# Attention items six deep with the multiplication on GpSimd, and constant matrix products in four kinds of stage

## The chip, the cores and the metric

The kernel runs on one core of one Trainium2 chip. A core has a matrix engine (TensorE, "PE" in the profile), a vector engine (VectorE, "DVE"), an activation engine (ScalarE, "ACT"), a general engine (GpSimd, "POOL") and a queue engine for transfers (SyncE, "SP"). The metric is the device time of one execution in microseconds (us).

## The reference

Two decoder blocks run one after the other on 256 latent tokens of width 1024. The first has two layers (mLSTM with gated linear attention, then RWKV-7, each with a convolutional FFN). The second has a layer of sparse attention with a SwiGLU FFN, and a layer of three-branch attention with a mixture of 8 experts. In both attention layers of the second block, each head does

```
s = q @ k.T * scale                  # 256 queries, up to 256 keys
p = softmax(where(mask, s, NEG))     # float32
o = p @ v
# three-branch layer: o = g0 * o_cmp + g1 * o_slc + g2 * o_win
# (cmp: up to 16 compressed keys; slc and win: up to 256 keys)
```

Everything is float32, with 16 query heads and 4 key/value heads of size 64. All other layers are projections, norms, scans and FFNs, float32 too.

## The kernel before

The program is a sequence of some 45 stages. Each stage is one block (`engines_block`, L204): every engine has its own instruction list, engines meet only by semaphores, and at the end of a block all engines wait for each other (the barrier is line L206).

`attention_stage` (L3653) is called twice: with one branch (16 items) in the sparse layer, and with three branches (48 items) in the other. An item is one query block of 128 rows, one pair of heads and one branch; query block b = 0 comes first for all pairs, and its items see at most 128 keys, those of b = 1 up to 256. The compressed branch has 16 keys in both. Each item passes through these steps:

- PE `score` (L3688): q times k for both heads into one of two PSUM pairs `SC`. It waits until the item two before has been read.
- VectorE `mask` (L3770, L3772): scale and add the mask into `scores` in SBUF, then the negated row maximum into `low`. The second waits for the first through a chain semaphore.
- ScalarE `expo` (L3747): exponential in place for each head, with the row sum into `total`.
- VectorE `norm` (L3780 to L3785): reciprocal of the sum, times the gate (three-branch layer), times a 0/1 mask for the compressed branch, then the whole row times the reciprocal.
- PE `turn` (L3699): transposes of the probabilities into PSUM.
- ScalarE `copy_turned` (L3732): PSUM to `pt`.
- PE `add` (L3711): probabilities times v, summed over branches in PSUM; ScalarE `copy_out` (L3738) stores the sum.

PE's order is written out: score(n), turn(n-2), add(n-3). VectorE's is mask(n), norm(n-1). `scores` has three slots, `low` and `total` have two. GpSimd has no work in the stage.

`norm_stage` (L935) computes an RMS norm, sometimes two in a row. PE sums squares (L1025), and after the reciprocal it spreads the result over all partitions (L1032); then VectorE, ScalarE and GpSimd scale (L1075, L1008, L1061, L1102). `row_stage` (L1426) is an output projection with weights that stream in whole rows; PE's products are L1468. `ffn_up_stage` (L2561) and `swiglu_stage` (L3798) are column projections whose products are L1330. In these three, PE's first product waits until ScalarE and VectorE have cut inputs and weights into two float32r parts.

`st.C("ones")` and `st.const` are constants that stay in SBUF. A plain float32 product gives two MATMUL records in the trace, a transpose one record, a float32r product one.

Of the kernel before, what the change touches and what calls it, by code (L numbers as in the profile page):

```python
# [934 lines left out]
def norm_stage(core, st, jobs, ahead=(), squares=None, early=None, late=None):  # L935
# [7 lines left out]
    with ExitStack() as ctx, core.engines_block() as block:  # L943
# [71 lines left out]
        def _(pe):  # L1015
            for j, job in enumerate(jobs):
# [17 lines left out]
                if j == 0 and late:  # L1034
                    late.multiply(pe)

# [80 lines left out]
        for turn in (early, late):  # L1117
            if turn:
                turn.settle()

# [305 lines left out]
def row_stage(core, st, g, T, rhs, lo, places, store, squares, squared, sums=(), ops_per_row=1.0, sums_from=0):  # L1426
# [7 lines left out]
    with ExitStack() as ctx, core.engines_block() as block:  # L1434
# [22 lines left out]
        def _(pe):  # L1457
            for k in range(K):
# [1102 lines left out]
def ffn_up_stage(core, st, weights, layer, T, sums, n_sums):  # L2561
# [10 lines left out]
    with weights.up_ctx as ctx, core.engines_block() as block:  # L2572
# [22 lines left out]
        @block.tensor  # L2595
        def _(pe):
            for n in range(len(g.tiles)):
                g.multiply(pe, n, x)
# [1054 lines left out]
def attention_stage(core, st, q, branches, out, ahead):  # L3653
# [13 lines left out]
    with ExitStack() as ctx, core.engines_block() as block:  # L3667
        begin_ahead(block, ahead)
        s = core.sb("scores", [P, 3, 2, LAT], ctx=ctx)
        low = core.sb("low", [P, 2, 2], ctx=ctx)  # L3670
        total = core.sb("total", [P, 2, 2], ctx=ctx)
        pt = core.sb("pt", [P, 2, 4, P], ctx=ctx)
        names = ("scored", "masked", "exped", "normed", "turned", "pt_ready", "summed", "out_taken")
        scored, masked, exped, normed, turned, pt_ready, summed, out_taken = (core.counter("at_" + n) for n in names)
        chain = core.counter("vector_chain")
# [4 lines left out]
        def _(pe):  # L3680
            def score(n):
                b, hp, i = items[n]
                br = branches[i]
                if n >= 2:
                    pe.wait_ge(masked.sem, masked.at(n - 1))
# [6 lines left out]
            def turn(n):  # L3692
# [4 lines left out]
                for h in (0, 1):  # L3697
                    for j, (at, w) in enumerate(branches[i].blocks(b)):
                        ins = nc.tensor.transpose(TR[n % 2][0:w, (h * 2 + j) * P:(h * 2 + j + 1) * P], s[:, n % 3, h, at:at + w], st.C("ident"))  # L3699
# [15 lines left out]
            for n in range(N + 3):  # L3715
                if n < N:
                    score(n)
                if 0 <= n - 2 < N:
                    turn(n - 2)
                if 0 <= n - 3:  # L3720
                    add(n - 3)

        @block.scalar
        def _(act):
# [15 lines left out]
            def expo(n):  # L3740
                b, hp, i = items[n]
                act.wait_ge(masked.sem, masked.at(n + 1))
                if n >= 2:
                    act.wait_ge(normed.sem, normed.at(n - 1))
                for h in (0, 1):
                    x = s[:, n % 3, h, 0:branches[i].keys(b)]
                    ins = nc.scalar.activation(x, x, ACT.Exp, bias=low[:, n % 2, h:h + 1], accum_out=total[:, n % 2, h:h + 1])  # L3747
                ins.then_inc(exped.sem, 1)

            for n in range(N + 4):  # L3750
                if 0 <= n - 2 < N:
                    copy_turned(n - 2)
                if n < N:
                    expo(n)
                if 0 <= n - 4 and (n - 4) % B == B - 1:
                    copy_out((n - 4) // B)

        @block.vector
        def _(dve):
            c = Chain(dve, chain)  # L3760

            def mask(n):
# [3 lines left out]
                x = s[:, n % 3, :, 0:K]  # L3766
                dve.wait_ge(scored.sem, scored.at(n + 1))
                if n >= 3:
# [902 lines left out]
```

## Time and profile before

| | us |
|---|---|
| median of 3 runs | 3501.94 (3500.34 to 3508.61) |
| the profiled execution | 3500.28 |
| its span in the profile | 3498.5 |

| engine | busy us | share |
|---|---|---|
| PE | 3126.0 | 89% |
| VectorE | 2504.4 | 72% |
| ScalarE | 1802.0 | 52% |
| GpSimd | 387.2 | 11% |

The busy time counts an instruction from its start to its end, with pipelined matmuls modelled. "PEclk" is the clock that TensorE was granted, as a share of full speed (1.00 is 2.4 GHz, 0.50 is 1.2 GHz). An "idle before" in brackets tells how long the engine stood before the instruction and whose event ended that. The costliest group in the whole program is the expert stage, some 980 us, in which the change has no line.

### The profile page before, as it was taken

To read this page: it belongs to the slowest core of one execution; us is meant where nothing else is said; L and a number is where in the kernel's file an instruction comes from. 1 tells how busy PE (TensorE), PEld (TensorE's weight loads), DVE (VectorE), ACT (ScalarE), POOL (GpSimd) and SP (SyncE) were. 2 spreads that over 40 slices of the span, in tenths; PEclk is the share of its full clock that TensorE was granted. 3 is DMA by queue.
4 is the path that set the end of the run, shared out by engine and by line. 5 is a ranking of instruction groups with operands and counts; after the bars stand their busy time and mean duration, and the time that the engine had idled before them with its cause. 6 is when DMAs were issued, how large, how long until landed. Compare 5 with 4: busy or idle time off the path is not lost. (4 is left out here: it accounts for less than half of the span.)

```text
span 3498.5 us, 67988 instructions
## 1 busy us (share of the span) xinstructions
PE 3126.0 (89%) x27208; PEld 2625.8 (75%) x27208; DVE 2504.4 (72%) x3881; ACT 1802.0 (52%) x3062; POOL 387.2 (11%) x370
## 2 busy tenths in 40 slices
PE   5998888999798898869987899888899999999997
PEld 3774457877673787759975898656789888988996
DVE  4867674449666445577857677566699999999997
ACT  2433233323313665435424444445588888878875
POOL 0000013431000221018300111000000000000000
PEclk8999889999899999979987999868899999999998
DMA  6530033428131000048730798300699999999995
GB/s 233 154 99 1 1 120 122 150 91 298 48 100 24 4 5 4 24 156 272 274 120 25 252 324 303 96 31 26 220 359 376 352 367 351 376 359 360 374 352 197
DMA packets 269600, 647.19 MB, mean 185 GB/s; under 512 B 25453, under 2 KB 123865, under 8 KB 269081
## 3 DMA queue, kind: packets, MB, share of 16 engines
q1 hardware_dynamic: 248457, 567.86, 45.7%
q0 software_dynamic: 20160, 73.41, 5.8%
q8 instruction: 188, 3.08, 0.4%
q10 hardware_dynamic: 720, 2.23, 0.2%
q14 instruction: 75, 0.61, 0.1%
HBM read 642.39 MB, written 1.05 MB: 184 GB/s over the span
## 5 line engine op out<-in xcount | busy, mean ns | idle before, releaser
L4435 DVE TENSOR_TENSOR weights_lo<-raw_ring,weights_hi 128x896 fp32r<-128x896 f32 (+1 forms) x376 | 413.3, 1126 | 50.7 <-ACT weights_hi L4388 40.9
L4388 ACT ACTIVATE weights_hi<-raw_ring 128x896 fp32r<-128x896 f32 (+1 forms) x376 | 366.9, 986 | 90.7 <-PE bank_pair L4358 89.3
L4358 PE MATMUL bank_pair<-weights_hi,expert_x_hi 128*128 128x448 f32 x1024 | 294.7, 369 | 5.1 <-DVE weights_lo L4435 5.1
L4358 PE MATMUL bank_pair<-weights_hi,expert_x_lo 128*128 128x448 f32 x1024 | 292.6, 367 | 0.0
L4358 PE MATMUL bank_pair<-weights_lo,expert_x_hi 128*128 128x448 f32 x1024 | 292.3, 367 | 0.0
L4435 DVE TENSOR_TENSOR weights_lo<-H,weights_hi 128x896 fp32r<-128x896 f32 (+1 forms) x240 | 264.5, 1133 | 23.6 <-ACT weights_hi L4388 14.7
L4388 ACT ACTIVATE weights_hi<-H 128x896 fp32r<-128x896 f32 (+1 forms) x240 | 236.8, 990 | 68.8 <-PE bank_pair L4358 68.8
L2652 DVE SCALAR_TENSOR_TENSOR conv<-bank_pair,vec,conv 128x189 f32<-128x189 f32 (+3 forms) x396 | 138.5, 428 | 146.5 <-ACT conv L2612 146.5
L4358 PEld LDWEIGHTS bank_pair<-weights_hi,expert_x_hi 128*128 128x128 f32 x1024 | 189.9, 188 | 21.4 <-issue 5.0
L4358 PEld LDWEIGHTS bank_pair<-weights_lo,expert_x_hi 128*128 128x128 f32 x1024 | 192.8, 188 | 16.6
L4358 PEld LDWEIGHTS bank_pair<-weights_hi,expert_x_lo 128*128 128x128 f32 x1024 | 192.9, 188 | 16.5
L1330 PE MATMUL bank_pair<-Y_parts,const_parts 128*128 128x256 f32 (+1 forms) x592 | 145.9, 330 | 9.3 <-DVE H_parts L1375 9.3
L344 PE MATMUL bank_pair<-x_hi,ring_hi 128*128 128x256 f32 (+1 forms) x352 | 117.5, 334 | 36.6 <-DVE x_lo L2769 16.4
L4358 PE MATMUL bank_pair<-weights_hi,hidden_hi 128*128 128x512 f32 x448 | 138.8, 391 | 0.0
L4358 PE MATMUL bank_pair<-weights_hi,hidden_lo 128*128 128x512 f32 x448 | 138.1, 390 | 0.0
L4358 PE MATMUL bank_pair<-weights_lo,hidden_hi 128*128 128x512 f32 x448 | 138.1, 389 | 0.0
L4435 DVE TENSOR_TENSOR weights_lo<-const,weights_hi 128x896 fp32r<-128x896 f32 (+1 forms) x120 | 133.2, 1132 | 2.6
L4388 ACT ACTIVATE weights_hi<-const 128x896 fp32r<-128x896 f32 (+1 forms) x120 | 119.0, 992 | 25.9 <-PE bank_pair L4358 25.3
L620 DVE SCALAR_TENSOR_TENSOR mod_sums_ada<-mod_ring_ada,act,mod_sums_ada 128x1024 f32<-128x1024 f32 x84 | 119.6, 1428 | 6.1 <-DMA mod_ring_ada<-in_w_ada 6.1
L1330 PEld LDWEIGHTS bank_pair<-Y_parts,const_parts 128*128 128x128 f32 x592 | 101.8, 190 | 21.2 <-DVE const_parts L1310 9.6
L1104 POOL TENSOR_SCALAR Y<-H,vec 128x256 f32<-128x256 f32 x2 | 1.8, 916 | 1046.5 <-DVE H L1075 1046.5
L344 PE MATMUL bank_pair<-x_lo,ring_hi 128*128 128x256 f32 (+1 forms) x352 | 115.9, 329 | 0.0
(798 smaller groups left out, 8302.0 us busy)
## 6 DMA issues: line engine op xcount, KB each, us to landing
raw_ring<-in_moe_w_gate SPq DMA_DIRECT2D x72, 896.0 KB, 6.9
raw_ring<-in_moe_w_up SPq DMA_DIRECT2D x64, 896.0 KB, 7.0
ring_up<-in_ffn_w_up SPq DMA_DIRECT2D x110, 512.0 KB, 4.3
raw_ring<-in_moe_w_down SPq DMA_DIRECT2D x48, 1024.0 KB, 7.3
mod_ring_ada<-in_w_ada POOLq DMA_DIRECT2D x84, 512.0 KB, 6.4
H<-in_moe_w_up SPq DMA_DIRECT2D x48, 896.0 KB, 7.1
ring_down<-in_ffn_w_down SPq DMA_DIRECT2D x66, 512.0 KB, 6.3
H<-in_moe_w_down SPq DMA_DIRECT2D x32, 1024.0 KB, 7.1
```

The source lines that it names most:

```text
L344: ins = self.core.nc.tensor.matmul(self.banks[o][:, 0:moving.shape[1]], lhs, moving, start=(s == self.first[o] and k == 0 and i == 0), sto ...
L620: ins = self.core.nc.vector.scalar_tensor_tensor(total, tile, scale, total, ALU.mult, ALU.add)
L1104: nc.gpsimd.tensor_scalar(job.dst(q)[:, h], work[j][:, q, h], job.scale(q, h), None, ALU.mult)
L1330: ins = self.core.nc.tensor.matmul(self.bank(it, o)[:, 0:T], w, y, start=s == self.begin[o] and k == 0 and a == 0, stop=s == self.end[o] a ...
L2652: ins = nc.vector.scalar_tensor_tensor(out, shifted, tap(w, 2 * it + o), out, ALU.mult, ALU.add)
L4358: ins = nc.tensor.matmul(banks[half][:, 0:b - a], x, w[:, a:b], start=start and i == 0, stop=stop and i == 2)
L4388: nc.scalar.activation(hi[:, u % CUTS, 0:n].bitcast(F32R), raw_part(u), ACT.Copy).then_inc(cut.sem, 1)
L4435: nc.vector.tensor_tensor(lo[:, u % CUTS, 0:n].bitcast(F32R), raw_part(u)[:, 0:n], hi[:, u % CUTS, 0:n], ALU.subtract).then_inc(parted.sem, 1)
```

## The change

Attention: six `scores` slots, four each of `low` and `total`. PE's order becomes score(n), turn(n-5), add(n-6). VectorE's order becomes shift(n), invert(n-2), lowest(n), gate(n-2), each with a semaphore of its own. The last multiplication goes to GpSimd. ScalarE copies the result out ahead of the exponential. For b = 0, a product of constants with 256 columns goes to PE ahead of each item's scores, into columns of the PSUM pair that are unused. Two products with 512 columns open the stage.

Elsewhere: a product of 512 columns opens the PE list of `row_stage`, `ffn_up_stage` and `swiglu_stage`; `jobs[-1].items // 2` of them end the PE list of `norm_stage` (2 for 256 tokens, 4 for 512). Nothing reads their results.

```diff
+def keep_busy(core, st, bank, n, cols=slice(0, 512)):
+    for _ in range(n):
+        core.nc.tensor.matmul(core.bank(bank)[:, cols], st.C("ones"), st.const[:, cols], start=True, stop=True)
...
@@ norm_stage, end of PE's list
+            keep_busy(core, st, 5, jobs[-1].items // 2)
...
@@ row_stage, ffn_up_stage, swiglu_stage, start of PE's list
+            keep_busy(core, st, 7, 1)
...
@@ attention_stage
-        s = core.sb("scores", [P, 3, 2, LAT], ctx=ctx)
-        low = core.sb("low", [P, 2, 2], ctx=ctx)
-        total = core.sb("total", [P, 2, 2], ctx=ctx)
+        TURN_LAG = 5
+        SLOTS, FACTORS, NORM_LAG = TURN_LAG + 1, 4, 2
+        s = core.sb("scores", [P, SLOTS, 2, LAT], ctx=ctx)
+        low = core.sb("low", [P, FACTORS, 2], ctx=ctx)
+        total = core.sb("total", [P, FACTORS, 2], ctx=ctx)
...
                 if n >= 2:
-                    pe.wait_ge(masked.sem, masked.at(n - 1))
+                    pe.wait_ge(shifted.sem, shifted.at(n - 1))
+                if b == 0:
+                    keep_busy(core, st, n % 2 * 2, 1, slice(256, 512))
...
-            for n in range(N + 3):
+            keep_busy(core, st, 7, 2)
+            for n in range(N + TURN_LAG + 1):
                 if n < N:
                     score(n)
-                if 0 <= n - 2 < N:
-                    turn(n - 2)
-                if 0 <= n - 3:
-                    add(n - 3)
+                if 0 <= n - TURN_LAG < N:
+                    turn(n - TURN_LAG)
+                if 0 <= n - TURN_LAG - 1:
+                    add(n - TURN_LAG - 1)
...
@@ scalar
-                if n >= 2:
-                    act.wait_ge(normed.sem, normed.at(n - 1))
+                if n >= FACTORS:
+                    act.wait_ge(normed.sem, normed.at(n - FACTORS + 1))
...
-            for n in range(N + 4):
-                if 0 <= n - 2 < N:
-                    copy_turned(n - 2)
+            for n in range(N + TURN_LAG + 2):
+                if 0 <= n - TURN_LAG < N:
+                    copy_turned(n - TURN_LAG)
+                if 0 <= n - TURN_LAG - 2 and (n - TURN_LAG - 2) % B == B - 1:
+                    copy_out((n - TURN_LAG - 2) // B)
                 if n < N:
                     expo(n)
-                if 0 <= n - 4 and (n - 4) % B == B - 1:
-                    copy_out((n - 4) // B)
...
@@ vector
+            for n in range(N + NORM_LAG):
+                if n < N:
+                    shift(n)
+                if n >= NORM_LAG:
+                    invert(n - NORM_LAG)
+                if n < N:
+                    lowest(n)
+                if n >= NORM_LAG:
+                    gate(n - NORM_LAG)
+
+        @block.gpsimd
+        def _(pool):
+            def norm(n):
+                b, hp, i = items[n]
+                br = branches[i]
+                K = br.keys(b)
+                x, r = s[:, n % SLOTS, :, 0:K], total[:, n % FACTORS]
+                pool.wait_ge(inverted.sem, inverted.at(n + 1))
                 if br.gate is not None:
+                    pool.wait_ge(gated.sem, gated.at(n_gated(n + 1)))
                 if br.some is not None:
+                    pool.wait_ge(kept.sem, kept.at(n_kept(n + 1)))
-                nc.vector.tensor_tensor(x, x, r.unsqueeze(2).to_broadcast([P, 2, K]), ALU.mult).then_inc(normed.sem, 1)
+                nc.gpsimd.tensor_tensor(x, x, r.unsqueeze(2).to_broadcast([P, 2, K]), ALU.mult).then_inc(normed.sem, 1)
+
+            for n in range(N):
+                norm(n)
```

`shift` is the first half of the old `mask` and `lowest` the second; `invert` and `gate` are the parts of the old `norm` without its last line.

## Rows read from the trace of the kernel before

**Rows 1.** Windows: busy us per engine (instructions), granted clock, DMA share, GB/s.

```profile
2300.00:2345.00 45.00, 42.63 (x228) 23.36 (x228) 31.44 (x129) 28.25 (x123) 0.00 (x0) 0.50 0.13 48
2345.00:2408.00 63.00, 50.96 (x352) 30.07 (x352) 45.35 (x133) 38.05 (x138) 0.00 (x0) 0.77 0.00 1
```

**Rows 2.** Waits from 2300 to 2408 us: total, times, longest.

```profile
ACT pt L3732 <- PE bank_pair L3699: 32.1, 45, 1.5
```

**Rows 3.** Timeline of PE, first block, second attention stage: start, length, instructions.

```profile
2312.30 0.80 PE L3688 MATMUL bank_pair<-k_slc,q 64*128 64x128 f32 x4
2313.03 0.69 PE L3699 MATMUL bank_pair<-const,scores 128*128 128x128 f32 x2
2313.64 0.70 PE L3711 MATMUL bank_pair<-pt,v_slc 128*64 128x128 f32 x4
2314.27 0.80 PE L3688 MATMUL bank_pair<-k_win,q 64*128 64x128 f32 x4
```

**Rows 4.** Timeline of PE, second block, second attention stage, clock 1.00.

```profile
2389.02 0.43 PE L3711 MATMUL bank_pair<-pt,vc 16*64 16x128 f32 x4
2389.38 0.70 PE L3688 MATMUL bank_pair<-k_slc,q 64*128 64x256 f32 x4
2390.01 0.66 PE L3699 MATMUL bank_pair<-const,scores 128*128 128x128 f32 x4
2390.60 0.66 PE L3711 MATMUL bank_pair<-pt,v_slc 128*64 128x128 f32 x8
2391.19 0.70 PE L3688 MATMUL bank_pair<-k_win,q 64*128 64x256 f32 x4
```

**Rows 5.** Timeline: where both attention stages start, change block and end.

```profile
1889.40 1.23 PE L3688 MATMUL bank_pair<-kd,q 64*128 64x128 f32 x8 [17.49 <-PEq L206]
...
1903.23 1.23 PE L3688 MATMUL bank_pair<-kd,q 64*128 64x256 f32 x4
...
1926.46 0.42 ACT L1371 ACTIVATE x_hi<-Y 128x256 fp32r<-128x256 f32 x1 [0.28 <-PEq L206]
...
2300.90 0.61 PE L3688 MATMUL bank_pair<-kc,q 64*128 64x16 f32 x4 [4.55 <-PEq L206]
...
2344.75 0.61 PE L3688 MATMUL bank_pair<-kc,q 64*128 64x16 f32 x4
...
2407.16 0.42 ACT L1371 ACTIVATE x_hi<-Y 128x256 fp32r<-128x256 f32 x1 [0.29 <-PEq L206]
```

**Rows 6.** Timeline of ScalarE and VectorE, second block, first attention stage.

```profile
1916.68 0.60 ACT L3732 ACTIVATE pt<-bank_pair 128x512 f32<-128x512 f32 x1 [0.26 <-PE bank_pair L3699]
...
1917.97 0.69 DVE L3770 SCALAR_TENSOR_TENSOR scores<-bank_pair,keep 128x512 f32<-128x512 f32 x1
...
1919.49 0.69 DVE L3785 TENSOR_TENSOR scores<-scores,total 128x512 f32<-128x512 f32 x1
1920.10 0.68 DVE L3770 SCALAR_TENSOR_TENSOR scores<-bank_pair,keep 128x512 f32<-128x512 f32 x1
```

**Rows 7.** GpSimd's products elsewhere: by form (count, busy, mean), and ns min/median/max.

```profile
L3240 POOL TENSOR_TENSOR kappa<-rw_k,kappa 128x256 f32<-128x256 f32 x16 | 11.7, 730 | 1.3
...
L1097 POOL TENSOR_TENSOR X<-X,H x6: 1272/1655/1665, 921.1 to 1775.3; 128x512 f32<-128x512 f32 x6
```

**Rows 8.** Weight loads between records of plain float32 products 512 wide; clock there.

```profile
428.66 0.34 PEld L2193 LDWEIGHTS bank_pair<-den,const 128*128 128x128 f32 x1 [0.52 <-issue]
429.51 0.34 PEld L2193 LDWEIGHTS bank_pair<-den,const 128*128 128x128 f32 x1 [0.52 <-issue]
...
427.70:430.00 2.30, 2.30 (x3) 1.11 (x4) 0.50 0.00 0
```

**Rows 9.** A norm's end, an ffn-up stage's first window, a row stage's first product.

```profile
1556.56 1.97 PE L1032 MATMUL bank_pair<-norm_root,const 128*128 128x64 f32 x8 [1.02 <-DVE norm_root L1044]
...
1562.00:1569.60 7.60, 5.06 (x24) 5.09 (x25) 5.20 (x11) 6.44 (x13) 1.93 (x1) 0.50 0.65 194
...
1928.27 0.55 PE L1468 MATMUL bank_pair<-x_hi,X_parts 128*128 128x256 f32 x1 [2.40 <-DVE X_parts L1499]
```

More of the change, by code:

```diff
@@ L3668, in attention_stage @@
         begin_ahead(block, ahead)
-        s = core.sb("scores", [P, 3, 2, LAT], ctx=ctx)
-        low = core.sb("low", [P, 2, 2], ctx=ctx)
-        total = core.sb("total", [P, 2, 2], ctx=ctx)
+        TURN_LAG = 5
[3 more added lines that the diff above has]
+        total = core.sb("total", [P, FACTORS, 2], ctx=ctx)
         pt = core.sb("pt", [P, 2, 4, P], ctx=ctx)
-        names = ("scored", "masked", "exped", "normed", "turned", "pt_ready", "summed", "out_taken")
-        scored, masked, exped, normed, turned, pt_ready, summed, out_taken = (core.counter("at_" + n) for n in names)
-        chain = core.counter("vector_chain")
+        names = ("scored", "shifted", "masked", "exped", "inverted", "gated", "normed", "turned", "pt_ready", "summed", "out_taken", "kept")
+        scored, shifted, masked, exped, inverted, gated, normed, turned, pt_ready, summed, out_taken, kept = (core.counter("at_" + n) for n in names)
+        n_gated = lambda n: sum(branches[i].gate is not None for _, _, i in items[:n])
+        n_kept = lambda n: sum(branches[i].some is not None for _, _, i in items[:n])
         SC = [core.psum[i].rearrange("p (h s) -> p h s", h=2) for i in (0, 1)]
@@ new lines, in shift, with lowest @@
+                nc.vector.scalar_tensor_tensor(s[:, n % SLOTS, :, 0:K], SC[n % 2][:, :, 0:K], HD ** -0.5, br.neg[:, b, 0:K].unsqueeze(1).to_broadcast([P, 2, K]),
+                                               ALU.mult, ALU.add).then_inc(shifted.sem, 1)
+            def lowest(n):
+                b, hp, i = items[n]
+                dve.wait_ge(shifted.sem, shifted.at(n + 1))
+                nc.vector.tensor_reduce(low[:, n % FACTORS], s[:, n % SLOTS, :, 0:branches[i].keys(b)], AX, ALU.max, negate=True).then_inc(masked.sem, 1)
@@ new lines, in invert, with gate @@
+            def invert(n):
+                b, hp, i = items[n]
+                br = branches[i]
+                r = total[:, n % FACTORS]
+                dve.wait_ge(exped.sem, exped.at(n + 1))
+                nc.vector.reciprocal(r, r).then_inc(inverted.sem, 1)
+            def gate(n):
+                b, hp, i = items[n]
+                br = branches[i]
+                r = total[:, n % FACTORS]
+                dve.wait_ge(inverted.sem, inverted.at(n + 1))
+                if br.gate is not None:
+                    nc.vector.tensor_tensor(r, r, br.gate[:, b, 2 * hp:2 * hp + 2], ALU.mult).then_inc(gated.sem, 1)
+                if br.some is not None:
+                    K = br.keys(b)
+                    x = s[:, n % SLOTS, :, 0:K]
+                    nc.vector.tensor_tensor(x, x, br.some[:, b, 0:K].unsqueeze(1).to_broadcast([P, 2, K]), ALU.mult).then_inc(kept.sem, 1)
```

33 lines of the change are left out of this document (11 added, 22 removed).

## The prediction

> **What bounds the kernel now.** I read the stage windows first, since the share of PE over the whole run mixes stages with different limits. Two stretches hold the attention stages. In them PE is busy nearly all the time while its granted clock is 0.50, the lower of its two levels (1.2 GHz), for the whole first block of queries of the second stage; over the second block it averages 0.77 [rows 1]. ScalarE's largest wait there is for PE's transposes, 32.1 us [rows 2]. So in the first block PE is the limit, at half its speed.
>
> The timeline of PE shows the cadence of one 128-key item: scores 0.73 us, transposes 0.61, product with v 0.63, then the next scores, 1.97 us together, none of them after a wait on another engine [rows 3]. At the upper level (2.4 GHz) the same line-up in the second block reads: a 4-record product 0.36, 256-wide scores 0.63, four transposes 0.59, an 8-record product 0.59 [rows 4]. There PE no longer leads: VectorE takes 2.13 us per item without a gap, of which the multiplication by the reciprocal sum is 0.61 (1919.49 to 1920.10), and ScalarE needs 1.87 of it, its 0.26 us wait taken off [rows 6]. The first attention stage runs from 1889.40 to 1926.46, its first 256-wide scores at 1903.23: 13.8 and 23.2 us. The second runs from 2300.90 to 2407.16, its second block from 2344.75: 43.9 and 62.4 us [rows 5].
>
> **The change, part by part.**
>
> *GpSimd multiplies.* VectorE loses 0.61 us per 256-key item (2.13 becomes about 1.5) and the wait between shift and minimum. GpSimd, idle here until now, gets 128x256 and 128x512 products. The nearest rows are 0.73 us for 128x256 and 1.27 to 1.66 us for 128x512 [rows 7]; I take 1.5. For a triple of the second block (16, 256 and 256 keys) that is about 0.4 + 2 x 1.5 = 3.4 us, at most 3.8, beneath what PE will need (below). So it leaves the path. If the cover were gone, a 128x512 product of 2.2 us or more would set the pace.
>
> *Six items deep.* The cycle scores, shift, minimum, exponential, reciprocal, product, transpose now has five items of slack, so PE finds its inputs ready. Its queue still holds all three steps in order: score(n), turn(n-5), add(n-6). The added waits are VectorE's on the shift of the same item (two instructions later, met) and GpSimd's on the reciprocal; behind GpSimd's stand only further products. What is late next is PE itself, with ScalarE close.
>
> *256-column constants in the first block.* 32 products, 8 + 24. Plain fp32 records 512 wide follow at 0.85 us (428.66 to 429.51) with clock 0.50, and a product is two such records [rows 8]: 512 columns cost 1.71 us at the lower level and 0.85 at the upper, 256 columns 0.85 and 0.43. They stand on PE's path: nothing hides them. What they may buy is the clock. At the upper level a 128-key item costs PE 0.42 (0.63 less 0.21 for 128 columns) + 0.37 (0.59 less two transposes at 0.11) + 0.36 = 1.15 us, plus 0.43 = 1.58, against 1.97 now. At the lower level it would be 1.97 + 0.85 = 2.82.
>
> *Opening of attention, 2 x 512 columns.* Nothing hides these either, as the first scores used to start 0.1 us after the barrier: 2 x 1.71 = 3.4 us twice. ScalarE's table load lies beside them.
>
> Second stage, at the upper level from shortly after the opening. First block: opening 3.5; five items with scores and constants only, 5 x 0.95; one with transposes, 1.2; 18 x 1.58 (the 16-key items somewhat less, so 1.52), 27.4; 1.5 for the first 3 us still at half speed. Sum 38.3 against 43.9, saves 5.6. Second block, per triple on PE: scores 0.37 + 0.63 + 0.63, transposes 0.37 + 0.59 + 0.59, products 0.36 + 0.59 + 0.59 = 4.72 us, or 1.57 per item; I take 1.6 since ScalarE needs nearly as much (1.87 twice and about 0.9 once, less two copies of the result at 0.25, 4.2 per triple). 24 x 1.6 - 1.5 (the first transposes still belong to short items) + 7.6 for draining six items = 44.5 against 62.4, saves 17.9. Together 23.5. First stage: first block 3.5 + 4.75 + 1.2 + 2 x 1.58 + 1.5 = 14.1 against 13.8, costs 0.3; second block 5 x 1.56 + 3 x 1.87 (ScalarE) + 7.7 = 21.1 against 23.2, saves 2.1. Attention saves 25.3 in all; I allow 2 us for hand-overs between engines of nearly equal pace, and take 23.
>
> *Stage openings* (row, ffn-up and swiglu stages, 512 columns). The row stage behind the first attention starts at 1926.4 and its first product at 1928.27, after a wait for VectorE's cut [rows 5, 9], so 1.71 us of constants fits; where it doesn't, 0.1 us is lost. The gain is a stage that starts at the upper clock. In the ffn-up stage from 1562.0 the clock is 0.50 for 7.6 us, PE working 5.06 of them [rows 9]: up to 2.5 us of gain, where the next tiles come in time. About ten stages qualify, but several start on saturated DMA. I take 6 us, bounds 0 and 12.
>
> *Norm ends* (512 columns, 2 or 4 times). PE's last spread matmuls end about 3.5 us before the next stage in the latent norms (1556.56 + 1.97 against 1562.0) [rows 9]. 2 x 1.71 us behind them end within some tenths of that, after which the drain follows: 0 to 0.4 us for each of seven norms at the lower clock (the same length of tail is in the other norms that feed a latent stage). I take 2, bounds 0 and 3.
>
> Sum: -23 - 6 + 2 = -27 us; the openings' gain is the least certain term, so I shade it to -26. The profiled execution took 3500.28 us (span 3498.5); it becomes 3474.3. The median of the runs shown is 1.7 us above that execution, so 3476.
>
> A rule of the Trainium skill speaks against the clock step. The rows show the clock low while PE issues transposes in a third of its steps [rows 1, 3]. "TensorE: Matmul & The Clock Gate", section Part 4 on PE-mode transpose, says that transposes don't count as activity for the clock. By that rule the new second block, with no constants in it, could fall back although PE is never idle; this is the first rival's mechanism. No row tells the two apart.
>
> The same product on GpSimd took from 1.27 to 1.66 us [rows 7]. "GPSIMD Engine Reference", section Specifications, puts contention down to VectorE instructions with two SBUF inputs. What VectorE keeps here reads one large SBUF input and PSUM, so by the rule the lower end holds; by the row, the upper. Either is under PE's 4.7 us per triple, so only the chance of the second rival moves.
>
> **The rivals.**
>
> 1. *The constants cost and the clock stays low* (slower). Mechanism: PE in the first blocks. For it: these stretches have held 0.50 for 44 us although PE never waits [rows 1, 3]. Against: the clock does rise once 256-wide scores come [rows 1], and the constants are denser than those. Price: 32 x 0.85 = 27 us, 7 us of openings, norm ends 2, while the second block keeps its present mixture and gains little, about 4: 3500 + 32 = 3534. It decides from the point where less than half of the first block runs at the upper level: half and half means (2.82 + 1.58) / 2 = 2.2 against 1.97, a loss of 7 us there.
>
> 2. *GpSimd or ScalarE sets the pace.* For it: [rows 6, 7], 1.87 and up to 1.66 against PE's 1.57. If every item of the second blocks took 1.9, 24 x 0.3 = 7 us of the gain go, with 2 in the short first items: 3485.
>
> 3. *The clock switches to and fro*, as it does now in the second block. First blocks give nothing or lose a little, second blocks gain 12, openings little: 3491 to 3500, say 3495.
>
> 4. *More than forecast*: openings and norms bring their full 12, and constants partly lie in waits. 3463.
>
> **How the numbers follow.** Forecast 0.62, its own range 3468 to 3484; rival 1 0.07, rival 2 0.11, rival 3 0.10, rival 4 0.10. The range from 3461 to 3494 leaves out rival 1, half of rival 3 and the far ends. A difference of 0.3% (10.5 us) is about what a measurement of this kernel tells from no change. Faster by more: the forecast, rivals 2 and 4 and a little of 3, 0.86. Within 0.3%: most of rival 3, 0.07. Slower: rival 1, 0.07.
>
> **What would show each step.** In the windows, PE's clock near 1.0 from a few us after each attention opening to its end; scores to scores about 1.5 to 1.6 us per item in both blocks of the second stage, and that stage about 83 us long; VectorE with waits for PE in the second block, where it now has none; GpSimd 128x512 products between 1.2 and 1.7 us. The openings are right if the 1562 stage's first tile passes PE in half the time. The prediction is wrong if a window of the first block still reads 0.50, or if GpSimd's products are what PE's transposes wait for.

## The result and the profile after

The changed kernel took 3476.44 us (median of 4 executions, 3468.64 to 3477.95), the kernel before 3505.28 us (4 executions): ratio 0.9915, interval 0.9898 to 0.9932. Measured again, beside three other versions, it took 3473.0 (6 executions) against 3502.16 (11), ratio 0.9905, interval 0.9888 to 0.9922. The ratios here and below are the recorded ones; the two medians alone give 0.9918 and 0.9917. The forecast was 3476, its range 3461 to 3494. The profiled execution took 3477.95 us (span 3476.1).

First the windows of the second attention stage after the change, to be held against [rows 1] (same columns): the opening, the rest of the first block with the first items of the second, and what follows.

```profile
2304.70:2308.70 4.00, 3.89 (x5) 1.85 (x6) 0.00 (x0) 1.28 (x1) 0.00 (x0) 0.50 0.66 220
2308.70:2345.00 36.30, 36.30 (x246) 20.18 (x244) 18.48 (x95) 24.80 (x114) 9.90 (x21) 1.00 0.09 35
2345.00:2389.00 44.00, 42.44 (x381) 25.65 (x382) 29.46 (x113) 37.31 (x145) 20.44 (x28) 1.00 0.01 2
```

The last but two column is the granted clock: 0.50 in the opening, then 1.00 to the end, where it was 0.50 and 0.77 before. PE is busy in 36.30 of 36.30 us and 42.44 of 44.00 us: the second block, where it was idle for 12 of 63 us, is now bound by PE too.

ScalarE's wait for PE's transposes, 32.1 us in [rows 2], is down to 8.1 (waits of the stage: total, times, longest):

```profile
ACT pt L3749 <- PE bank_pair L3715: 8.1, 20, 0.8
```

PE's cadence in the first block, against [rows 3] (start, length, instruction):

```profile
2328.64 0.70 PE L1128 MATMUL bank_pair<-const 128*128 128x256 f32 x2
2329.27 0.49 PE L3704 MATMUL bank_pair<-k_win,q 64*128 64x128 f32 x4
2329.70 0.39 PE L3715 MATMUL bank_pair<-const,scores 128*16 128x128 f32 x2
2330.01 0.44 PE L3727 MATMUL bank_pair<-pt,v_win 128*64 128x128 f32 x4
2330.38 0.70 PE L1128 MATMUL bank_pair<-const 128*128 128x256 f32 x2
```

From constant to constant it is 1.74 us, where an item took 1.97. In it the constant takes 0.63 us (2328.64 to 2329.27) and the kernel's own work 1.11 (1.16 where the transposes are of 128 keys). Next the second block, against [rows 4]:

```profile
2364.31 0.70 PE L3704 MATMUL bank_pair<-k_slc,q 64*128 64x256 f32 x4
2364.94 0.66 PE L3715 MATMUL bank_pair<-const,scores 128*128 128x128 f32 x4
2365.53 0.66 PE L3727 MATMUL bank_pair<-pt,v_slc 128*64 128x128 f32 x8
2366.11 0.70 PE L3704 MATMUL bank_pair<-k_win,q 64*128 64x256 f32 x4
```

One 256-key item follows the other in 1.80 us, with no step waiting. VectorE over the same time (against [rows 6], in brackets the idle time before and what ended it):

```profile
2365.06 0.69 DVE L3784 SCALAR_TENSOR_TENSOR scores<-bank_pair,seen 128x512 f32<-128x512 f32 x1 [0.81 <-PE bank_pair L3704]
2365.66 0.15 DVE L3797 RECIPROCAL total<-total 128x2 f32<-128x2 f32 x1
2365.78 0.69 DVE L3790 TENSOR_REDUCE low<-scores 128x2 f32<-128x512 f32 x1
2366.39 0.15 DVE L3805 TENSOR_TENSOR total<-total,gates 128x2 f32<-128x2 f32 x1
2366.86 0.69 DVE L3784 SCALAR_TENSOR_TENSOR scores<-bank_pair,seen 128x512 f32<-128x512 f32 x1 [0.33 <-PE bank_pair L3704]
```

It has no large multiplication any more, and it waits for PE's scores, 0.81 and 0.33 us here. GpSimd's products (against [rows 7]; groups by form over both attention stages, with count, busy us and mean ns):

```profile
L3833 POOL TENSOR_TENSOR scores<-scores,total 128x512 f32<-128x512 f32 x24 | 25.0, 1042 | 13.0 <-DVE total L3805 9.6 <-DVE total L3797 3.4
L3833 POOL TENSOR_TENSOR scores<-scores,total 128x256 f32<-128x256 f32 x24 | 14.7, 614 | 129.6 <-DVE total L3797 112.6 <-DVE total L3805 17.1
```

Where each attention stage starts and ends, against [rows 5]. Each fence shows the first constant product of a stage: the first attention stage, the row stage behind it, the second attention stage:

```profile
1890.63 1.19 PE L1128 MATMUL bank_pair<-const 128*128 128x512 f32 x1 [17.25 <-PEq L206]
```

```profile
1925.78 1.10 PE L1128 MATMUL bank_pair<-const 128*128 128x512 f32 x2 [0.62 <-PEq L206]
```

```profile
2304.81 1.19 PE L1128 MATMUL bank_pair<-const 128*128 128x512 f32 x1 [5.33 <-PEq L206]
```

From barrier to barrier the first attention stage went from 37.1 to 35.2 us and the second from 106.3 to 84.1: 24.1 us less. In a second profile of the changed kernel they are 35.2 and 84.0.

The first 7.6 us of the ffn-up stage that began at 1562.0, against [rows 9]:

```profile
1567.60:1575.20 7.60, 6.36 (x44) 5.59 (x45) 5.20 (x11) 7.25 (x14) 1.92 (x1) 0.97 0.64 195
```

There are 44 records (two of them the constant's) instead of 24, and a clock of 0.97 instead of 0.50; the stage is 2.1 us shorter, 133.6 for 135.7. Not all of this can be booked for the constants: over the profiles of this study that have them both here and at the end of the norm ahead, the stage takes 133.6 us in seven and 135.0 in four, and it takes 134.9 in constants_only, which has neither.

Stages without an edit differ between profiles too: the one from 1136.8 takes 343.9 us before, 346.4 after, and from 335.9 to 346.4 over all profiles of this study. All stages but the two of attention add up to 3355.1 us before and 3356.9 after, and to anything from 3339.8 to 3365.0 over the 14 profiles. So the total of one execution doesn't settle 5 us. Below, stages are compared one by one, and the totals that carry an argument are those of several executions.

### The profile page after: what moved, and what is told of

Its sections match the earlier page's. It is cut to its first block and busy times, and to the rows that moved or that the text cites. A ratio compares the mean times of both kernels' runs of the same rounds, so it can differ in the third digit from the quotient of the medians.

```text
span 3476.1 us, 68320 instructions
## 1 busy us (share of the span) xinstructions
PE 3149.8 (91%) x27352; PEld 2620.2 (75%) x27352; DVE 2464.0 (71%) x3817; ACT 1799.4 (52%) x3062; POOL 431.4 (12%) x434
## 5 line engine op out<-in xcount | busy, mean ns | idle before, releaser
L4483 DVE TENSOR_TENSOR weights_lo<-raw_ring,weights_hi 128x896 fp32r<-128x896 f32 (+1 forms) x376 | 413.2, 1125 | 51.0 <-ACT weights_hi L4436 41.3
L4436 ACT ACTIVATE weights_hi<-raw_ring 128x896 fp32r<-128x896 f32 (+1 forms) x376 | 366.9, 986 | 91.1 <-PE bank_pair L4406 89.5
L4483 DVE TENSOR_TENSOR weights_lo<-H,weights_hi 128x896 fp32r<-128x896 f32 (+1 forms) x240 | 264.4, 1132 | 23.3 <-ACT weights_hi L4436 14.3
L344 PE MATMUL bank_pair<-x_hi,ring_hi 128*128 128x256 f32 (+1 forms) x352 | 117.9, 335 | 26.6 <-DVE x_lo L2780 12.9
L1128 PE MATMUL bank_pair<-const 128*128 128x512 f32 (+1 forms) x144 | 82.4, 689 | 45.4 <-PEq L206 45.4
```

Source lines behind the costliest of these rows:

```text
L344: ins = self.core.nc.tensor.matmul(self.banks[o][:, 0:moving.shape[1]], lhs, moving, start=(s == self.first[o] and k == 0 and i == 0), sto ...
L1128: core.nc.tensor.matmul(core.bank(bank)[:, cols], st.C("ones"), st.const[:, cols], start=True, stop=True)
L4436: nc.scalar.activation(hi[:, u % CUTS, 0:n].bitcast(F32R), raw_part(u), ACT.Copy).then_inc(cut.sem, 1)
L4483: nc.vector.tensor_tensor(lo[:, u % CUTS, 0:n].bitcast(F32R), raw_part(u)[:, 0:n], hi[:, u % CUTS, 0:n], ALU.subtract).then_inc(parted.sem, 1)
```

## The experiments

Lengths are from barrier to barrier in the profiled execution, in us. "First" and "second" are the two attention stages. The constants in the other stages are in all versions but the kernel before and constants_only; one_opening and no_norm_ends leave out some or all of the norm ends.

| kernel | depth | product on | constants in attention | first | second |
|---|---|---|---|---|---|
| before | 3 | VectorE | none | 37.1 | 106.3 |
| constants_only | 3 | VectorE | both | 39.1 | 107.1 |
| old_depth | 3 | GpSimd | both | 39.5 | 114.5 |
| three_deep | 3 | GpSimd | both | 75.7 | 229.2 |
| multiply_on_vector | 6 | VectorE | both | 36.6 | 88.3 |
| after, and again | 6 | GpSimd | both | 35.2, 35.2 | 84.1, 84.0 |
| no_first_block | 6 | GpSimd | opening | 32.2 | 93.1 |
| no_opening | 6 | GpSimd | ahead of scores | 45.4 | 116.9 |
| no_constants, no_constants_5 | 6 | GpSimd | none | 34.8, 36.5 | 83.7, 89.6 |
| one_opening | 6 | GpSimd | first stage's opening | 32.2 | 83.4 |
| no_norm_ends | 6 | GpSimd | first stage's opening | 32.2 | 89.5 |
| rest_only | 3 | VectorE | none | 38.2 | 110.7 |

**no_first_block: openings without the constants ahead of the scores.**

```diff
-                if b == 0:
-                    keep_busy(core, st, n % 2 * 2, 1, slice(256, 512))
```

> Changed kernel without the 256-column constants ahead of the first block's scores (opening pair kept). The second attention stage took 84.1 us with them. Theory A, the constants must be there all along the first block: the clock drops to 0.50 soon after the opening and PE's 128-key cadence is again 1.9 us or more, so 18 x (1.95 - 1.74) = 4 us longer, 88 us or above. Theory B, once the clock is up, PE's own dense work holds it: no constants to pay, each of 24 items 0.5 to 0.6 us shorter, stage at 71 to 74 us, clock 1.0 throughout. First attention stage, 35.2 us with them: A 35 to 37, B 31 to 32.

One execution: 3470.75 us; first stage 32.2, second 93.1. (The kernel before took 3494.89 beside this one, no_opening, no_constants and multiply_on_vector, one execution each.) The windows of the second stage, from its start:

```profile
2287.00:2291.00 4.00, 3.95 (x8) 1.44 (x8) 0.00 (x0) 1.28 (x1) 0.00 (x0) 0.50 0.65 226
2291.00:2295.00 4.00, 3.23 (x31) 2.28 (x32) 3.53 (x18) 2.97 (x17) 0.85 (x2) 0.93 0.73 300
2295.00:2346.00 51.00, 50.45 (x256) 26.74 (x256) 24.06 (x116) 32.29 (x142) 14.49 (x27) 0.50 0.00 1
```

The opening did lift the clock (0.93), and then it fell and stayed at 0.50 for 51 us in which PE was busy for 50.45. So in the 48-item stage it took the constants ahead of the scores to hold the clock (one profile without them, all profiles of six-deep kernels with both kinds at 1.00). In the 16-item stage it didn't: without them that stage is 3.0 us shorter, in this profile and in two more below.

**no_opening: only the constants ahead of the scores.**

```diff
-            keep_busy(core, st, 7, 2)
             for n in range(N + TURN_LAG + 1):
```

> Changed kernel without the two 512-column constants at the attention opening, those in the first block kept. Theory A (the first block's constants alone raise the clock): the clock is up within some 5 to 7 us, the stage saves the 3.4 us of the opening and pays up to 2.5 us for more work at half speed: 81 to 84 us. Theory B (the opening is what raises it): the clock stays at 0.50 over the first block at 2.8 us per item, stage over 105 us. First attention stage 32 to 35 by A, over 43 by B.

One execution took 3504.66 us, all of the gain gone; first stage 45.4, second 116.9. Its windows:

```profile
2297.10:2343.00 45.90, 45.87 (x174) 23.92 (x176) 13.60 (x69) 19.37 (x84) 7.32 (x15) 0.50 0.12 47
2343.00:2413.90 70.90, 69.64 (x452) 38.66 (x452) 34.74 (x139) 44.68 (x173) 22.93 (x33) 0.72 0.00 1
```

The same constants that held the clock at 1.00 left it at 0.50 when it started there, and then cost more, at the lower clock: 1.15 us each (2326.43 to 2327.58) for 0.63. This is the mechanism of the prediction's first rival, and it comes true when the opening is absent. Its price was too high: it had the total 32 us above the kernel before, and here it is 10, since the second block, which it had gaining 4 us, takes 51.2 for 62.4 even so.

**no_constants: depth and GpSimd alone.**

```diff
-                if b == 0:
-                    keep_busy(core, st, n % 2 * 2, 1, slice(256, 512))
...
-            keep_busy(core, st, 7, 2)
```

> Changed kernel with no constants in attention at all, only the order six deep and the multiplication on GpSimd. Theory A (constants are needed for the clock in the first block): clock 0.50 over it at 1.9 us per item, 44 us for it as before, and second block at about 1.55 us: 43 us; stage 87 us, first attention stage 35 us. Theory B (PE kept fed is enough to raise it): clock rises inside the first block, stage under 78 us.

One execution took 3465.55 us, with stages of 34.8 and 83.7: as short as with the constants. The same kernel again:

> The changed kernel without any constants inside attention (no opening, none ahead of first-block scores); the other stages keep theirs. Theory 1 (the gain is depth and GpSimd; the constants in attention pay for their own time and no more): the attention stages come to 34 to 36 and 83 to 86 us, and the whole is level with the changed kernel within 4 us, either side, ratio to before 0.990 to 0.992. Theory 2 (they cost more than they bring, as one look of 3465.6 suggests): 6 to 10 us below the changed kernel, ratio 0.988 to 0.990. Theory 3 (they hold the clock on most executions and one look missed the bad ones): 5 us or more above the changed kernel, ratio 0.993 or more.

3475.57 us (5 executions), ratio 0.9912, interval 0.9896 to 0.9928, level with the changed kernel. The stages in its profile took 36.5 and 89.6. These are two profiles of one kernel, 6 us apart in one stage. The windows of the second stage, in the first profile and then in the other:

```profile
2292.50:2337.00 44.50, 44.15 (x234) 24.46 (x236) 21.83 (x110) 29.88 (x133) 11.74 (x24) 0.50 0.14 48
2337.00:2376.20 39.20, 37.88 (x344) 23.08 (x342) 25.97 (x100) 33.04 (x125) 18.59 (x24) 0.99 0.01 2
```

```profile
2297.70:2333.00 35.30, 35.01 (x191) 20.09 (x192) 17.23 (x91) 24.74 (x111) 9.63 (x20) 0.50 0.16 60
2333.00:2387.20 54.20, 52.92 (x388) 30.30 (x386) 30.71 (x117) 38.77 (x146) 20.62 (x28) 0.78 0.01 2
```

PE in the first of the two profiles, in the first block and where the second block begins:

```profile
2310.18 0.80 PE L3702 MATMUL bank_pair<-k_slc,q 64*128 64x128 f32 x4
2310.91 0.69 PE L3713 MATMUL bank_pair<-const,scores 128*128 128x128 f32 x2
2311.52 0.70 PE L3725 MATMUL bank_pair<-pt,v_slc 128*64 128x128 f32 x4
2312.15 0.80 PE L3702 MATMUL bank_pair<-k_win,q 64*128 64x128 f32 x4
...
2330.93 0.61 PE L3702 MATMUL bank_pair<-kc,q 64*128 64x16 f32 x4
```

An item of the first block takes 1.97 us (2310.18 to 2312.15), exactly as in [rows 3]: depth doesn't speed it. The block's scores are done after 38.4 us all the same (2292.5 to 2330.93, and 38.4 in the other profile), where the kernel before takes 43.9. Mostly that is because the transposes and products of three items more than before (three at 1.24 us) are put off into the second block, and PE stands 0.2 us at the start instead of 1.4. With constants the block takes 41.3. The second block then takes 45.3 us in one profile (to the end at 2376.2) and 51.2 in the other, by when the clock rises: 44.9 or 58.7 us after the stage began, which is 6.5 or 20.3 us into the block. It takes 42.8 in the changed kernel, with constants, and 62.4 in the kernel before. So constants cost 2.9 us in the first block and give 2.5 to 8.4 in the second, and the stage comes out at 84.1 and 84.0 with them, 83.7 and 89.6 without. What depth brings, beyond work put off, lies in the second block.

**multiply_on_vector: depth and constants, with the product back on VectorE.**

```diff
+                nc.vector.tensor_tensor(x, x, r.unsqueeze(2).to_broadcast([P, 2, K]), ALU.mult).then_inc(normed.sem, 1)
...
-                nc.gpsimd.tensor_tensor(x, x, r.unsqueeze(2).to_broadcast([P, 2, K]), ALU.mult).then_inc(normed.sem, 1)
```

> Changed kernel with the multiplication by the reciprocal sums on VectorE again, behind the gate, rest as it is. Theory A (taking it off VectorE matters in the second block): VectorE then needs about 3.9 + 2 x 0.61 + 0.2 = 5.3 us per triple against PE's 4.6, so the second block grows by 8 x 0.7 = 5 to 6 us, stage 89 to 90 us; first block unchanged. Theory B (depth alone did it, VectorE has room): stage within 1 us of 84.1.

One execution took 3491.72 us; the stages are 1.4 and 4.3 us longer than in the changed kernel. VectorE in the second block:

```profile
2385.23 0.68 DVE L3784 SCALAR_TENSOR_TENSOR scores<-bank_pair,seen 128x512 f32<-128x512 f32 x1
2385.83 0.15 DVE L3797 RECIPROCAL total<-total 128x2 f32<-128x2 f32 x1
2385.94 0.69 DVE L3790 TENSOR_REDUCE low<-scores 128x2 f32<-128x512 f32 x1
2386.55 0.15 DVE L3805 TENSOR_TENSOR total<-total,gates 128x2 f32<-128x2 f32 x1
2386.73 0.69 DVE L3816 TENSOR_TENSOR scores<-scores,total 128x512 f32<-128x512 f32 x1
2387.34 0.68 DVE L3784 SCALAR_TENSOR_TENSOR scores<-bank_pair,seen 128x512 f32<-128x512 f32 x1
```

There is no gap: VectorE sets 2.11 us per 256-key item (2385.23 to 2387.34) against PE's 1.80. So VectorE's relief is worth 5.7 us in both stages together.

**constants_only: the kernel before with attention's constants.**

```diff
+                if b == 0:
+                    keep_busy(core, st, n % 2 * 2, 1, slice(256, 512))
...
+            keep_busy(core, st, 7, 2)
             for n in range(N + 3):
```

> The kernel before, with the attention constants alone: two 512-column products open the stage and one of 256 columns stands ahead of each first-block score. Order, slots and VectorE's multiplication are as before. Theory 1 (the 24 us come from depth and from the multiplication on GpSimd; constants buy a clock that here PE cannot use): the clock is near 1.00, but second block stays at VectorE's 2.13 us per 256-key item and the first block at 1.8 us or more, so the second attention stage takes 98 to 106 us (106.3 before), the first 37 to 39 (37.1 before), and the whole is 0 to 8 us below the kernel before. Theory 2 (the clock alone carries much of the gain): second stage 90 to 95 us, first 35 or less, whole 13 us or more below. Theory 3 (constants cost and the clock stays at 0.50): second stage over 120 us.

One execution: 3506.61 us, where the kernel before took 3491.14 to 3510.76 (17 executions), stages 39.1 and 107.1. The second stage's windows behind its opening:

```profile
2309.20:2345.00 35.80, 34.46 (x234) 18.75 (x233) 25.90 (x105) 23.20 (x103) 0.00 (x0) 1.00 0.09 35
2345.00:2412.00 67.00, 53.95 (x393) 31.95 (x392) 49.69 (x152) 41.51 (x153) 0.00 (x0) 0.85 0.00 1
```

The clock is 1.00 and 0.85 and the stage isn't shorter. In the second block PE is busy in 54 of 67 us and VectorE in 50, so neither is full. They wait for each other (waits from 2310 to 2400: total, times, longest; L3711 is the transposes, L3798 the product on VectorE, L3783 the shift, L3700 the scores):

```profile
PE bank_pair L3711 <- DVE scores L3798: 10.4, 12, 1.3
DVE scores L3783 <- PE bank_pair L3700: 21.7, 27, 5.1
```

That is the chain of one item. In the first block the higher clock pays for the constants and no more: 45.4 us for 43.9. So the clock bought with constants is worth nothing to the stage as a whole (the old form without them takes 106.3 us here and 110.7 in a second profile), which is the first of the expectation's theories, a little beyond its ranges (98 to 106 us, and a total 0 to 8 us below the kernel before).

**three_deep and old_depth: the changed kernel with three slots.** The first only cuts the turn lag; the second also takes the reciprocal one item behind the shift.

```diff
-        TURN_LAG = 5
+        TURN_LAG = 2
...
-        SLOTS, FACTORS, NORM_LAG = TURN_LAG + 1, 4, 2
+        SLOTS, FACTORS, NORM_LAG = TURN_LAG + 1, 4, 1
```

> The changed kernel with a turn lag of 2 in place of 5, so three score slots as in the kernel before; GpSimd's multiplication, the split waits and the constants stay. Theory 1 (depth is what lets PE run without waits, since the chain shift, minimum, exponential, reciprocal, product of one item now has two more hand-overs): PE waits for GpSimd's product at the transposes, 2.1 us or more per item of the second block, second attention stage 95 to 105 us against 84.1, first 37 to 40 against 35.2, whole 3488 to 3500. Theory 2 (taking the multiplication off VectorE was enough, depth is spare): second stage 84 to 87 us, whole within 5 us of the changed kernel.

One execution took 3666.75 us, far outside both theories; the stages take 75.7 and 229.2. VectorE, GpSimd and PE in the second stage show why:

```profile
2419.82 0.42 DVE L3784 SCALAR_TENSOR_TENSOR scores<-bank_pair,seen 128x256 f32<-128x256 f32 x1 [4.05 <-PE bank_pair L3704]
...
2420.91 0.61 POOL L3833 TENSOR_TENSOR scores<-scores,total 128x256 f32<-128x256 f32 x1 [4.38 <-DVE total L3805]
2421.58 0.69 PE L3715 MATMUL bank_pair<-const,scores 128*128 128x128 f32 x2 [1.81 <-POOL scores L3833]
...
2422.82 1.22 PE L1128 MATMUL bank_pair<-const 128*128 128x256 f32 x2
...
2423.97 0.80 PE L3704 MATMUL bank_pair<-k_win,q 64*128 64x128 f32 x4
...
2424.82 0.42 DVE L3784 SCALAR_TENSOR_TENSOR scores<-bank_pair,seen 128x256 f32<-128x256 f32 x1 [4.05 <-PE bank_pair L3704]
```

Read it as a ring: the shift of one item lets VectorE go on to the reciprocal two items back, then GpSimd multiplies, PE transposes, adds, issues the constant and the next scores, and the next shift can start, 5.00 us later. With a reciprocal two items behind and a transpose two items behind, every item closes this ring alone. PE is busy in 142 of the stage's 229 us, and its clock is 0.51 over them, constants or not, so PE's own part of the ring, 3.2 of the 5.0 us here, runs at the lower level too.

> The changed kernel with the depth of the kernel before: turn lag 2 (three score slots) and the reciprocal one item behind the shift, in place of two; GpSimd's multiplication and all constants stay. With the turn lag alone cut to 2 the second attention stage took 229 us, 4.8 us per item, since score(n), shift(n), reciprocal(n-2), product(n-2), transposes(n-2) and score(n+1) made one loop. Here that loop spans two items. Theory 1 (depth carries most of the gain; GpSimd alone, with a chain longer by two hand-overs, brings little): about 2.0 to 2.3 us per item, second attention stage 96 to 110 us, first 38 to 41. Theory 2 (the 229 us came from the order alone, and GpSimd with the old depth is as good as with six items): second stage 84 to 89 us, first 35 to 37.

One execution took 3510.48 us (the kernel before beside it 3504.99), stages 39.5 and 114.5: the first theory, and a little beyond its range in the second stage (96 to 110 was expected). Even with a fit order, GpSimd at the old depth gains nothing; a transpose in the second block still comes behind a wait for the product:

```profile
2399.15 1.11 PE L3715 MATMUL bank_pair<-const,scores 128*128 128x128 f32 x4 [1.27 <-POOL scores L3833]
```

With constants in all four, the table makes a square: three slots and VectorE 107.1, three slots and GpSimd 114.5, six and VectorE 88.3, six and GpSimd 84.1. The step to six is worth 30 us with the product on GpSimd, where lags and slots alone differ. With it on VectorE it is worth 19, but there the three-slot kernel also has the old order on VectorE and the old waits (PE waits for the minimum and not for the shift), and no run parts these from the depth. GpSimd is worth 4 us with depth. That it costs 7 without is not shown: the clock over the second block was 0.69 there for 0.83 in constants_only, and the next experiment shows what such a difference does to that block.

**rest_only: the openings and norm ends elsewhere, with the attention stage of before.** In code, `attention_stage` is put back.

> The changed kernel with the old attention stage: only the 512-column products at the starts of row, ffn-up and swiglu stages and at the ends of the norms are added to the kernel before. The prediction's terms for them: 6 us gained by openings, 2 us lost at norm ends, together 4 us faster. Theory 1 (stage lengths of one profile: openings gain 8 to 9 us in ffn-up, row and router stages, norm ends cost 5, the norm whose 512-column pair starts behind a late product alone 3.9): 1 to 6 us faster, ratio 0.998 to 1.000. Theory 2 (the openings' gain in that profile was chance, the norm ends' cost is not): 2 to 6 us slower, ratio 1.0005 to 1.002.

It took 3495.13 us (12 executions) against 3500.57 (17), ratio 0.9978, interval 0.9964 to 0.9993: 0.0022 x 3500 = 7.7 us faster, between 2 and 13 (5.4 by the two medians). The sign is that of the first theory, the size at the upper end of its 1 to 6 us or a little beyond. Its attention stages, with the same instructions as before, took 38.2 and 110.7 us for 37.1 and 106.3. The difference is in the second blocks: 66.8 us at a mean clock of 0.68 in the second stage, where the kernel before has 62.4 at 0.77. So one profile of the old form is uncertain by 5.5 us in both stages together, and attention's gain may be that much higher than the 24.1 above.

**one_opening and no_norm_ends: versions meant to beat both.** Both have depth and GpSimd, and the opening only in the attention stage with one branch. The first leaves the norm ends out where a norm has a `late` product, the second leaves them all out.

```diff
-            keep_busy(core, st, 5, jobs[-1].items // 2)
+            if not late:
+                keep_busy(core, st, 5, jobs[-1].items // 2)
...
+            if B == 1:
+                keep_busy(core, st, 7, 2)
```

> A version meant to beat both: no constants ahead of scores, the opening only in the first attention stage (one branch), and no constants at the ends of those norms that hold a late product (the one from 2165.1 lost 3.9 us to them). Sum from stage lengths against the changed kernel: first attention 32.2 for 35.2, second about as now, that norm 14 for 17.7, so 6 to 7 us less: 3468 to 3471 where the changed kernel stands at 3476, ratio to before 0.989 to 0.991. Rival: those stage lengths were the clock's chance in single profiles, and the version is level with the one without constants in attention.

> The same, with no constants at the end of any norm. If they only cost (stage lengths: 1.1 us ahead of swiglu, 3.9 in the late norm, 0.1 to 0.5 elsewhere), this is 1 to 2 us below the version that keeps them in the other norms. Rival: they keep the clock for the stage behind, and this one is 2 us or more above it.

> The changed kernel itself on the same chip as the three versions above, for a direct comparison: ratio to before 0.990 to 0.993, as in the first measurement.

Against 3502.16 us for the kernel before: one_opening 3474.25, ratio 0.9914 (0.9896 to 0.9932); no_norm_ends 3479.63, 0.9926 (0.9912 to 0.994); the changed kernel 3473.0, 0.9905 (0.9888 to 0.9922). None beats it, and the intervals don't part the three. Nothing bears out the expectation that norm ends only cost. That the norm from 2165.1 had lost 3.9 us to its constants was wrong: it takes from 13.8 to 20.6 us over the profiles, and 17.5 in one_opening, which has none there. What norm ends bring shows in the ffn-up stage from 534.3. It takes 250.97 or 250.98 us in all ten profiles with constants at the end of the norm ahead of it, and 253.27 in the four without them, two of which have the stage's own opening. The window of its first 4 us, after:

```profile
539.71:543.71 4.00, 2.30 (x7) 1.35 (x8) 3.25 (x6) 3.91 (x7) 0.00 (x0) 1.00 0.53 157
```

and in one_opening:

```profile
532.56:536.56 4.00, 3.25 (x5) 1.55 (x6) 3.25 (x6) 3.91 (x7) 0.00 (x0) 0.50 0.59 161
```

With the norm end the stage begins at 1.00; with the opening alone it is at 0.50, as before. So the gain booked for the opening belongs here to the norm's end. Half of it is lost again in the next stage (from 787.6), which takes 128.9 us in the same ten profiles and 127.7 to 127.9 in the four: the two stages together gain 1.0 to 1.3 us.

## Why the prediction was right, step by step

- **What bounds.** The reading was right for the first block (PE, without waits, at half clock) and half right for the second. There the rows were read as VectorE's pace; at three slots it was just as much the chain of one item, since constants_only keeps 107.1 us with PE idle for 13 of 67 us and VectorE for 17. [rows 1] had the sign of it: VectorE, the third figure, is busy in 45.35 of 63 us.
- **First blocks.** Second stage: 41.3 us (2304.7 to the second block's first scores at 2346.03) against 38.3 forecast. The forecast saving of 5.6 was 2.6. The term that was too small is the 256-column constant, 0.63 us and not 0.43: 24 x 0.2 = 4.8 us. Halving for the columns was the step that failed; halving for the clock was right, as records with 512 columns follow each other at 0.43 us at clock 1.00 (940.31 to 940.74, a norm's end) and 0.85 at 0.50. The item's own work was 1.11 us, for which 1.15 was worked out. Against it stands the 1.5 us for work at half speed, which came to nothing: the clock is 1.00 from 2308.8, before the first scores. The opening took 3.8 us of the stage for 3.5, as no_first_block shows (2286.97 to the scores at 2290.74); in the changed kernel the first scores come 0.6 us later, behind the first item's constant. First stage: 14.3 against 14.1.
- **Second blocks.** They took 42.8 us against 44.5, and 20.8 against 21.1. Three items take 4.62 us on PE (4.72 worked out), and ScalarE, busy for 37 of 44 us, does not hold it up.
- **GpSimd.** It took 1.04 us for 128x512, below both ends of the rows it was taken from (1.27 and 1.66), and 0.61 for 128x256 (0.73). It lies beneath PE's pace, as said, and it did not matter for the sum. The Trainium skill, "GPSIMD Engine Reference", section Specifications, puts contention down to VectorE instructions with two SBUF inputs or in a 2-port mode. The large ones of the first kind are absent here, and no run tells of the second; the trace agrees with the lower end that followed from it, and lies below that. No run isolates the cause.
- **Attention in all.** It gained 24.1 and 24.2 us in the two profiles, for 25.3 worked out and 23 taken.
- **What brings it.** Here the prediction was right in size and partly off in reason. It gave the first block's saving to the clock that the constants buy. The runs show that block as long at 0.50 without constants (38.4) as was forecast at 1.00 with them (38.3). Its sum for the second block, PE at 4.72 us per triple instead of a chain that waits, is what holds: 17.9 us forecast, 19.6 measured with constants, 11 to 17 without. Without constants in the second stage the clock rises by itself in its second block, 5.8 and 6.5 us after that block began in two profiles (stage 83.4 and 83.7 us) and 20.0 and 20.3 us after in two (89.5 and 89.6). In the mean of these few profiles the constants are worth 2 to 3 us in the second stage. In the first, the opening alone gives 32.2 us in three profiles, no constants 34.8 and 36.5, both kinds 35.2. In the totals (0.9905 and 0.9915 with them, 0.9912 without) the constants in attention don't show.
- **Openings and norm ends.** The prediction took 6 gained and 2 lost, net 4; measured are 7.7, between 2 and 13, which contains it. The split was wrong. In the ffn-up stage from 534.3 norm ends gain 2.3 us (and the stage behind loses 1.2), and the opening alone gains none. In the row stages behind attention it is the clock at the stage's start that decides: the first takes 26.6 us in constants_only without an opening, where it starts at 1.00, and the second 28.3 in old_depth with one, where it starts at 0.50.
- **The total.** That it came within 1 us of the forecast is luck in part. The second stage's first block missed its term by 3.0 us, its second block beat it by 1.7, and the other stages beat theirs by 1 to 4; the other stages of one execution alone vary by 25 us.
- **Rivals.** The first, clock down and constants paid for, happened in no_opening (3504.66), two products per stage away from the changed kernel; no_first_block shares its low clock without its constants. In the changed kernel's two profiles it did not happen. (Its sum, 3500 + 32, is 3532; 3534 goes with the median of 3502.) The second had GpSimd or ScalarE at 1.9 us for every item; they stayed below PE's pace. The third, a clock that switches, is what constants_only and old_depth show (0.83 and 0.69 over the second block), not the changed kernel.
- **The transposes.** The Trainium skill, "TensorE: Matmul & The Clock Gate", section Part 4, says that transposes don't count as PE activity in the same way, and that the full clock doesn't engage for them. The changed kernel's second block holds 1.00 for 44 us with transposes as every third step, so that rule didn't bring the clock down there; it may have a part in the 51 us at 0.50 of no_first_block, which no run separates.

Still open is why the same first-block constants hold the clock from 1.00 and don't lift it from 0.50, and whether an opening alone in the first attention stage, both kinds in the second, and all norm ends would save the 3.0 us that the first stage shows (32.2 against 35.2). That version was not run.

## What to carry to other kernels

Before pricing an engine's relief or a faster clock, follow the ring of semaphores: with three slots neither made the stage shorter (107.1 and 114.5 us, for 106.3 and 110.7 in the old form), and with six the chain stopped being the limit, so that GpSimd's relief brought 4 us. Vary the slots together with the order written out on each engine, since a lag that doesn't fit the slots makes a ring of its own (229 us for 84). When constants are added for the clock, check what the clock does at the start of the stretch and whether the stage is shorter at all, and take several executions: one kernel's attention stage had two lengths here (83.7 and 89.6 us), by when the clock rose.

## What the runs showed of the hardware

- A plain float32 product of constants with 256 columns takes 0.63 us from its start to the next start at clock 1.00 and 1.15 at 0.50 (no_opening), more than half of the 0.85 and 1.71 for 512 columns. The opening's two with 512 columns take 3.7 us at 0.50 up to the first scores (no_first_block, 2287.05 to 2290.74), for 3.4 from [rows 8].
- The clock fell to 0.50 and stayed there for 51 us while PE was busy in 50.45 of them (no_first_block), and under the same instructions as the changed kernel's, less its two opening products, it stayed at 0.50 for the whole first block, 65.8 us (no_opening).
- Without constants the clock rose in the second block after 5.8 to 6.5 us or after 20.0 to 20.3 us, two profiles each, and then stayed at 1.00 to the stage's end. In the three-slot kernels constants_only and old_depth, with PE idle for 13 of 67 and 12 of 69 us, it fell again and again.
- GpSimd's product with a broadcast second operand took 1.04 us for 128x512, where its products of two full operands took 1.27 to 1.66 [rows 7]. Which of operand and neighbour makes the difference was not tried.
